# Merge stage of a mixer layer: gate scaling on GpSimd, and the weight split moved ahead of the merged tile

## What is computed

```
g_a, g_b, g_c = jnp.split(jax.nn.sigmoid(h @ w_gate), 3, axis=-1)
merged = g_a * (o_a @ w_br_a) + g_b * (o_b @ w_br_b) + g_c * (o_c @ w_br_c)
return merged @ w_out
```

## Time and profile before

| | |
|---|---|
| median of 3 runs | 3554.07 us (3553.71 to 3555.38) |
| the profiled execution | 3556.05 us, span 3554.5 us |
| PE busy | 3493.2 us, 98% of the span |
| DVE busy | 1942.9 us, 55% |
| ACT busy | 1472.2 us, 41% |
| POOL busy | 174.6 us, 5% |
| merge stage, first layer | 785 to 874 us |
| merge stage, second layer | 1259.4 us later, the same pattern |

### The profile page before, as it was taken

One profiled execution on the slowest core, in us unless ns is written; L12 is line 12 of the kernel. 1 busy time (PEld: TensorE's weight loads), 2 busy tenths in 40 slices (PEclk: granted clock), 3 DMA queues, 4 the chain that ended last, 5 costly groups with the idle time before them and its releaser, 6 DMA issues.

```text
span 3554.5 us, 46476 instructions
## 1 busy us (share of the span) xinstructions
PE 3493.2 (98%) x16692; PEld 2775.4 (78%) x16692; DVE 1942.9 (55%) x3249; ACT 1472.2 (41%) x2210; POOL 174.6 (5%) x181
## 2 busy tenths in 40 slices
PE   9999999999999999999999999999999999999997
PEld 7888886667888888888866578888887777878886
DVE  5443466767544344434657675443378776645433
ACT  5432355654444234423456544442233434434421
POOL 0000000000000000000000001000000001020001
PEclk9999999999999999999999999999999999999999
DMA  4233422114322332235221053223422223313231
GB/s 142 95 100 105 158 98 72 42 58 159 139 94 100 102 101 95 94 105 164 91 80 54 28 172 139 94 95 106 141 95 83 78 75 104 116 62 104 96 105 65
DMA packets 99831, 356.06 MB, mean 100 GB/s; under 512 B 11823, under 2 KB 12079, under 8 KB 98920
## 3 DMA queue, kind: packets, MB, share of 16 engines
q1 hardware_dynamic: 83232, 300.16, 25.2%
q10 hardware_dynamic: 9416, 30.34, 2.6%
q0 software_dynamic: 7040, 23.66, 1.8%
HBM read 330.98 MB, written 26.80 MB: 101 GB/s over the span
## 4 chain that ended last, share of the span: by engine, by line
PE 89%; DVE 6%; ACT 3%; issue 2%; POOLq 0%; DMA 0%; POOL 0%; ACTq 0%; DVEq 0%; SPq 0%
PE bank L325 25%; PE bank L327 24%; PE bank L326 24%; PE bank L618 5%; PE bank L1102 1%; PE bank L1073 1%; PE bank L1748 1%; PE bank L1082 1%; DVE unit_lo L304 1%; PE bank L1721 1%; ACT unit_hi L299 1%; PE bank L1177 1%; PE bank L1737 1%; PE bank L1119 1%; PE bank L1164 1%
## 5 line engine op out<-in xcount | busy, mean ns | idle before, releaser
L304 DVE TENSOR_TENSOR unit_lo<-unit_raw,unit_hi 128x1024 fp32r<-128x1024 f32 x526 | 647.4, 1233 | 693.0 <-ACT unit_hi L299 682.6
L325 PE MATMUL bank<-h_hi,unit_hi 128*128 128x512 f32 x2416 | 956.2, 396 | 5.7 <-DVE h_lo L409 4.1
L327 PE MATMUL bank<-h_hi,unit_lo 128*128 128x512 f32 x2416 | 943.1, 390 | 0.0
L326 PE MATMUL bank<-h_lo,unit_hi 128*128 128x512 f32 x2416 | 942.6, 390 | 0.0
L299 ACT ACTIVATE unit_hi<-unit_raw 128x1024 fp32r<-128x1024 f32 x526 | 552.9, 1053 | 355.2 <-PE bank L327 342.6
L325 PEld LDWEIGHTS bank<-h_hi,unit_hi 128*128 128x128 f32 x2416 | 455.0, 188 | 115.3 <-issue 22.1
L327 PEld LDWEIGHTS bank<-h_hi,unit_lo 128*128 128x128 f32 x2416 | 454.7, 188 | 96.5
L326 PEld LDWEIGHTS bank<-h_lo,unit_hi 128*128 128x128 f32 x2416 | 455.2, 188 | 92.8 <-issue 1.7
L325 PE MATMUL bank<-act_hi,unit_hi 128*128 128x512 f32 x880 | 346.7, 394 | 0.0
L327 PE MATMUL bank<-act_hi,unit_lo 128*128 128x512 f32 x880 | 345.0, 392 | 0.0
L326 PE MATMUL bank<-act_lo,unit_hi 128*128 128x512 f32 x880 | 341.5, 388 | 0.0
(11 more groups left out here) (325 smaller groups left out, 4540.9 us busy)
## 6 DMA issues: line engine op xcount, KB each, us to landing
unit_raw<-in_units SPq DMA_DIRECT2D x564, 512.0 KB, 3.3
gates_kept<-gate_z POOLq DMA_DIRECT2D x32, 256.0 KB, 2.3
sig_ab<-gates_kept ACTq DMA_DIRECT2D x16, 512.0 KB, 3.6
bias_rows<-bias_once POOLq DMA_DIRECT2D x2, 3840.0 KB, 20.7
x_kept<-x ACTq DMA_DIRECT2D x3, 2048.0 KB, 11.0
x<-x_kept ACTq DMA_DIRECT2D x3, 2048.0 KB, 8.6
xc<-xc ACTq DMA_DIRECT2D x16, 256.0 KB, 4.4
bias_t<-bias_rows POOLq DMA_DIRECT2D x16, 256.0 KB, 3.7
```

Source lines behind the costliest of these rows:

```text
L304: nc.vector.tensor_tensor(w_lo[u % SLOTS][:], raw[u % SLOTS][:], w_hi[u % SLOTS][:].bitcast(F32), ALU.subtract).then_inc(unit_lo, 1)
L325: nc.tensor.matmul(out_ap, w_h, r_h, start=first, stop=False)
L326: nc.tensor.matmul(out_ap, w_h, r_l, start=False, stop=False)
L327: return nc.tensor.matmul(out_ap, w_l, r_h, start=False, stop=last)
```

## The change

`scale_ab` leaves DVE. POOL now scales the eight pairs, at the start of its merge program (`mix3_pool`), each as soon as it has landed; POOL's clearing of `ssq` comes behind them. And where a unit follows a branch unit, its weight split is made earlier in written order: ACT runs `split_hi` of the unit u+4 between the sigmoid of the pair and the rounding of the merged tile, and DVE runs `split_lo` of the same unit between `val` and `m_lo`, instead of at the head of the next unit.

```
         for u in range(MERGE_UNITS):
             kind, m = MERGE_ORDER[u]
-            split_hi(act, r, u + AHEAD)
+            if u == 0 or MERGE_ORDER[u - 1][0] == "c":
+                split_hi(act, r, u + AHEAD)
...
+            if u + 1 < MERGE_UNITS:
+                split_hi(act, r, u + 1 + AHEAD)
             act.wait_ge(s["m_val"], m + 1)
             nc.scalar.activation(tile(m_hi, m), val[0][:], ACT.Copy).then_inc(s["m_hi"], 1)
...
         for u in range(MERGE_UNITS):
             kind, m = MERGE_ORDER[u]
-            split_lo(dve, r, u + AHEAD)
+            if u == 0 or MERGE_ORDER[u - 1][0] == "c":
+                split_lo(dve, r, u + AHEAD)
             if kind == "c":
-                if m == 2:
-                    scale_ab(0)
                 if m > 0:
                     gate_c(m)
                 continue
...
             nc.vector.tensor_tensor(val[0][:], part[0][:], sig_c[m % 3][:], ALU.add).then_inc(s["m_val"], 1)
+            if u + 1 < MERGE_UNITS:
+                split_lo(dve, r, u + 1 + AHEAD)
             dve.wait_ge(s["m_hi"], m + 1)
             nc.vector.tensor_tensor(tile(m_lo, m), val[0][:], tile(m_hi, m).bitcast(F32), ALU.subtract).then_inc(s["m_lo"], 1)
-            if m + 1 < KD:
-                scale_ab(m + 1)
...
     def mix3_pool(pool, f):
         fence(pool, f)
+        for m in range(KD):
+            pool.wait_ge(s[f"sig_in{m % 2}"], 16 * (m // 2 + 1))
+            ab = sig_ab[m % 2][:].rearrange("p (e t) -> p e t", e=2)
+            nc.gpsimd.tensor_tensor(ab, ab, rs_full[:].unsqueeze(1).to_broadcast([P, 2, S]), ALU.mult).then_inc(s["ab_scaled"], 1)
         nc.gpsimd.memset(ssq[:], 0.0).then_inc(s["ssq_add"], 2)
```

More of the change, by code:

```diff
@@ L1565, in mix3_dve @@
     def mix3_dve(dve, f, r, gn_col):
[L1567 to L1570, removed]
         def gate_c(m):
```

## The result

| | before | changed |
|---|---|---|
| median of 11 runs | 3555.38 us (3553.46 to 3557.52) | 3564.36 us (3561.22 to 3567.62) |
| the profiled execution | 3556.05 us, span 3554.5 | 3564.53 us, span 3562.9 |

The ratio is 1.0024, with a 95% interval of 1.0016 to 1.0032: slower by 9.0 us, where 5.0 had been predicted.

The account below looks back on a forecast made before the run. PE was taken as the bound in mid-merge, with waits on DVE at its end. Per layer 3.97 us lost at the start less 1.46 gained at the end, 5.0 in both, on 3554.07 gave 3559.1 us; range 3549 to 3563.

Parts of the forecast that it names:

- DVE's own work: Late merges: DVE free 5.00 us after a merge starts, under PE's 5.49, so PE sets the pace of merges 5 to 7.
- the moved splits: In the merge: cost nothing, since PE needs each of these weights at least two units (11 us) later.
- POOL's product: One 128x1024 product on POOL, length P: 2.46 us, between 2.26 and 2.55.
- the rival of a slow product: POOL's product takes longer, loss over 7.1 us from P over 2.8; 3563.5 us at P = 3.2; chance 0.14.
- what it does to DVE: Two-operand SBUF instructions on DVE and POOL block each other whole; each POOL product pushes a DVE row back 2.28 us.
- P - 0.18: Push on a DVE row by one POOL product of length P between two instructions; 2.28 us predicted.
- DVE's row did not hold out: Rival at merge start: POOL gets its turn only at DVE's next pause, PE doesn't wait at b0; 3551.1 us, chance 0.18.
- two products got in, not one: Row of `o_lo`: predicted case, both get in, 3559.1 us, chance 0.50; rival, only one gets in, 3554.5, chance 0.10.
- Start of the merge: Ahead of b0: POOL's first two products delay its split to 797.24, so PE starts b0 3.97 us late per layer.
- Middle: Middle of the merge: POOL's products meet weight splits with two units in hand and cost nothing.
- End of the merge: Around the output product: first wait stays, 0.36 us later; second wait goes; 1.46 us gained per layer.
- Sum: Both merges: 3.97 lost less 1.46 gained, 2.5 us lost per layer, 5.0 in both; 3559.1 us.

Follow-up runs that it names:

- e2: Kernel before with only the weight splits in the new order, DVE still scaling the pairs; 3556.02 us against 3556.64, ratio 1.0000.
- e7: Changed kernel, with POOL's second product held until all eight low parts of the attention output are there; 3556.85 us against 3555.45 before, ratio 1.0006.
- e4: Changed kernel, with POOL waiting for all eight low parts and each pair's load issued ahead of the rounding; 3549.70 us against 3556.64 before, ratio 0.9982.
- e5: Kernel before plus eight extra DVE subtractions ahead of the split for b0, POOL doing nothing; 3565.76 us against 3555.44, ratio 1.0028.
- e6: Kernel before plus four extra DVE subtractions ahead of the split for b0; 3555.90 us against 3555.44, ratio 1.0003.
- e1: Kernel before with POOL scaling all pairs, weight splits left in the old order; 3563.83 us against 3556.64, ratio 1.0021.
- e8: Changed kernel with each pair's load issued earlier, ahead of the rounding, and nothing else; 3559.07 us against 3555.45 before, ratio 1.0011.
- e3: Changed kernel, with POOL waiting for all eight low parts of the attention output before its first product; 3555.92 us against 3556.64 before, ratio 0.9996.
- e9: Changed kernel, POOL waiting for all low parts and scaling seven pairs, DVE scaling the eighth behind tile 6's `m_lo`; 3550.17 us against 3555.45 before, ratio 0.9986.

## Why the prediction was off

**Right: DVE's own work, the moved splits.** Merge 6 and merge 5 of the changed kernel start 5.49 us apart (860.78 to 866.27), as PE lets them, and the moved splits alone don't change the time (e2).

**Right: POOL's product.** 2.41 us, where 2.46 was taken; the rival of a slow product, from 2.8 on, falls.

**Right: what it does to DVE.** One waits for the other's whole instruction. P - 0.18 gives 2.23 per product; the row shows 2.21 for two (8.12 - 3.70 = 4.42) and 2.21 for one (e7). The Trainium skill's rule in "SBUF — State Buffer", section "Who interferes with whom", holds here for two-operand DVE instructions, and so does its other half, that a DVE instruction with one SBUF input does not contend: three products at 0.68 us beside POOL in e4. DVE's row did not hold out, and two products got in, not one, as the predicted case had it.

**Start of the merge: the failed step.** The prediction priced PE's lateness, 3.97 us, and took it that PE then goes on at its pace. Measured are 3.48 us of lateness and 1.6 us more in which PE works at the lower clock: 5.1 us. The latency from the split to PE was put at 0.40, by the one from `m_lo`; it is 0.05 (798.47 to 798.52), and 0.04 in e7 (792.02 + 1.22 to 793.28). That makes up 0.35 of the 0.49 by which the lateness was over. The missing term is the clock, 1.6 us per layer at the start (1.1 over the prediction, once the 0.49 is taken off). The earlier trace rows gave no hint of it: waits of 1.66 and 1.72 us, with the clock at full behind them. But the same trace of before has a wait about as long ahead of the merge, with the clock near its lower level behind it, and the same again in the second layer (1.78 us at 2000.90):

```profile
741.51 0.50 PE L1177 MATMUL bank<-val_r,tri_r 128*128 128x512 f32 x1 [1.77 <-DVE sb_lo L1365]
```

```profile
742.00:744.00 2.00, 2.00 (x10) 1.79 (x10) 1.43 (x5) 0.82 (x2) 0.00 (x0) 0.57 0.34 131
744.00:746.00 2.00, 2.00 (x11) 0.71 (x8) 0.78 (x3) 0.00 (x0) 0.00 (x0) 0.58 0.00 0
```

The prediction did not draw on these rows, and put the slow stretch behind a wait of 4 us at nothing without a reason. e5 brings it about with DVE alone, e6 and e7 take it away by a shorter wait.

**Middle: right.** Four of POOL's products met splits, which took 2.57 to 2.85 us in place of 1.22 and held nobody up: PE is 6.43 us later than in before at the end of b0 (798.52 + 7.09 against 793.67 + 5.51) and 6.40 at the start of b5 (855.07 against 848.67).

**End of the merge: right in the first layer, not in the second.** The first wait stays, 0.33 us later for 0.36 predicted, and the second goes, 1.95 us. Net 1.62 for the 1.46 predicted, and 1.72 - 1.58 = 0.14 in the second layer, where the clock fell behind the wait of 1.91 us, too:

```profile
2136.16 0.64 PE L325 MATMUL bank<-m_hi,unit_hi 128*128 128x512 f32 x1 [1.91 <-DVE m_lo L1603]
```

```profile
2136.00:2138.00 2.00, 1.84 (x5) 1.47 (x6) 1.97 (x4) 0.00 (x0) 0.00 (x0) 0.59 0.75 262
2138.00:2140.00 2.00, 2.00 (x7) 1.59 (x6) 1.27 (x3) 0.87 (x2) 0.00 (x0) 0.56 0.00 0
```

**Sum.** Predicted 3.97 - 1.46 = 2.5 per layer. Measured 3.48 + 1.58 - 1.62 = 3.4 in the first and 3.48 + 1.67 - 0.14 = 5.0 in the second, together 8.4. Of the 3.4 us that the prediction is short of this (8.4 less 5.0), the clock behind long waits makes 1.58 + 1.67 + 1.58 = 4.8; the start, less late than predicted by 0.49 in each layer, takes back 1.0, and the end, clock aside, 0.4. Without the clock the merges would have lost 3.6 us, 1.4 less than predicted. Of the 5.3 us between the measured 3564.36 and the predicted 3559.1, 1.3 are the higher median of before; 3.4 are the merges, and 0.6 the rest that they don't hold. The case that the prediction had for a loss this large, a slow product of POOL, is not what happened.

## What to carry to other kernels

A wait of PE can cost more than its length: price the slow stretch behind it too (about 1.6 us here), unless PE would have to wait again soon behind it, as in e2. Look at the granted clock in the windows behind every wait of PE in the trace at hand, not only behind those that the change touches. Work moved from DVE to POOL was free here only where it didn't meet a row of DVE instructions with two SBUF operands that somebody waits for; the idle time of POOL is not the measure, the place of its instructions is. Here a load issued 1.5 us earlier and one wait that keeps POOL out of a row of seven instructions turned a loss of 9 us into a gain of 7.

## What the runs showed of the hardware

The clock and PE's waits: behind waits of 3.3 to 3.7 us the granted clock fell to its 1.2 GHz level in all eight cases (changed kernel, e1, e5, e8, two layers each), at a price of 1.4 to 2.6 us in b0. Behind waits of 1.91 to 2.12 us it fell in six of eight (changed, e2, e3, e7), in two kernels in one layer and not in the other. Behind the shorter waits of the merges, 0.45 to 1.72 us (before, e1, e4 to e9), it never fell. But behind the wait of 1.77 or 1.78 us at about 741 and 2001 us, which all eleven profiles have, it fell in 13 of 22 cases. So the length of a wait alone doesn't decide it. The Trainium skill, "TensorE: Matmul & The Clock Gate", Part 1, ties the clock to how busy PE has been and says that the moment of a change varies with a window that runs free of the kernel; that fits a fall in one layer and none in the other, but no run here tests it.

Where DVE's instructions with two SBUF operands and POOL's products were both queued, they took turns, one instruction each: POOL's first product got in behind an `o_lo` in progress (to 790.49), then came the stretched `o_lo` (to 793.31), then POOL's second product (to 795.57), then the next `o_lo`. So two products cost two pushes of 2.21 us. The latency from a DVE result to PE was 0.04 to 0.05 us for the split ahead of b0 (changed, e5, e6, e7), and 0.40 for `m_lo` (before, changed); why they differ was not looked into.
